# Attention: scaling the exponentials on GpSimd before they are transposed, in place of transposed inverse sums

## What is computed

```
def _masked_softmax(s, mask):
    p = jax.nn.softmax(jnp.where(mask, s, NEG), axis=-1)
    return p * mask.astype(p.dtype)
...
o = g[:, :, 0] * o_cmp + g[:, :, 1] * o_sel + g[:, :, 2] * o_win      # o_sel, o_win: softmax(q k - alibi) v
...
s = (einsum(q_nope, k_nope) + einsum(q_rope, k_r)) * scale             # latent attention
pr = _masked_softmax(s, s_idx[None, :] <= tq[:, None])
return jnp.einsum('bhqs,bshd->bqhd', pr, v)
...
merged = gm[:, :, 0] * (o_nsa @ w_br_nsa[i]) + gm[:, :, 1] * (o_mla @ w_br_mla[i])
```

## Time and profile before

| | |
|---|---|
| median of 3 runs | 1554.8 us (1554.15 to 1554.89) |
| the profiled execution | 1554.5 us, its span 1552.7 us (1.8 us lie around the span) |
| TensorE busy | 1508.3 us, 97% of the span |
| VectorE, ScalarE, GpSimd busy | 665.6, 513.5 and 473.8 us |
| attention loop, first scores of unit 1 to the first merge matmul | 131.09 to 251.28 us from the span's start |

### The profile page before, as it was taken

The page is one execution under the profiler, slowest core; times in us unless marked ns, Lnnn a source line. Parts: engine busy times, 40 slices in busy tenths (PEclk is TensorE's granted clock), DMA queues, the critical chain, the costliest instruction groups (busy, mean ns, idle before and its releaser), DMA issues.

```text
span 1552.7 us, 19377 instructions
## 1 busy us (share of the span) xinstructions
PE 1508.3 (97%) x7613; PEld 1020.4 (66%) x7614; DVE 665.6 (43%) x1102; ACT 513.5 (33%) x917; POOL 473.8 (31%) x249
## 2 busy tenths in 40 slices
PE   8999999999999999999999999999999999998997
PEld 6975667888878888888888777458544343443443
DVE  4155666213643333333343668673633232332334
ACT  4236666222453333331245432524111111111112
POOL 3440125444534444444714355542101000010000
PEclk9999999999999999999999999999999999999999
DMA  8233001222242222222223322257999999999996
GB/s 323 101 117 94 1 2 41 96 95 95 74 143 96 95 95 95 96 99 102 97 82 107 118 76 88 108 197 291 361 430 427 431 422 428 430 429 413 429 426 255
DMA packets 51051, 306.87 MB, mean 198 GB/s; under 512 B 6921, under 2 KB 7177, under 8 KB 38288
## 3 DMA queue, kind: packets, MB, share of 16 engines
q1 hardware_dynamic: 46288, 292.03, 48.0%
q0 software_dynamic: 4096, 11.49, 1.9%
q10 hardware_dynamic: 576, 2.10, 0.3%
HBM read 303.39 MB, written 4.19 MB: 198 GB/s over the span
## 4 chain that ended last, share of the span: by engine, by line
PE 80%; DMA 10%; DVE 5%; ACT 2%; issue 2%; POOL 1%; SPq 0%; ACTq 0%; DVEq 0%; POOLq 0%
PE banks L420 19%; PE banks L465 12%; PE banks L1226 11%; PE banks L423 9%; DMA ring<-experts 8%; PE banks L1270 4%; PE banks L1279 2%; PE banks L445 2%; PE banks L1034 2%; PE banks L2402 2%; PE banks L2483 1%; DMA arena<-experts 1%; PE banks L2418 1%; PE banks L892 1%; PE banks L2389 1%
## 5 line engine op out<-in xcount | busy, mean ns | idle before, releaser
L383 POOL TENSOR_TENSOR arena_r<-ring,arena_r 128x1024 fp32r<-128x1024 f32 x144 | 355.5, 2474 | 411.6 <-ACT arena_r L368 392.1
L368 ACT ACTIVATE arena_r<-ring 128x1024 fp32r<-128x1024 f32 x144 | 151.6, 1058 | 441.0 <-PE banks L423 279.1
L420 PE MATMUL banks<-hT_r,arena_r 128*128 128x512 f32 x640 | 250.0, 391 | 0.0
L420 PE MATMUL banks<-arena_r 128*128 128x512 f32 x640 | 249.1, 389 | 0.0
L1226 PE MATMUL banks<-ring,arena 128*64 128x512 f32 x704 | 222.8, 606 | 14.8 <-DMA ring<-experts 14.7
L465 PE MATMUL banks<-arena_r 128*128 128x512 f32 x784 | 183.5, 389 | 0.6 <-DVE arena_r L410 0.6
L465 PEld LDWEIGHTS banks<-arena_r 128*128 128x128 f32 x784 | 147.1, 188 | 31.5 <-POOL arena_r L383 1.0
L1226 PEld LDWEIGHTS banks<-ring,arena 128*64 128x64 f32 x704 | 70.5, 139 | 145.4 <-issue 144.9
L420 PEld LDWEIGHTS banks<-hT_r,arena_r 128*128 128x128 f32 x640 | 120.1, 188 | 29.0 <-issue 3.4
L420 PEld LDWEIGHTS banks<-arena_r 128*128 128x128 f32 x640 | 120.1, 188 | 25.1 <-issue 0.2
L1894 DVE TENSOR_TENSOR resid<-resid,banks 128x1024 f32<-128x1024 f32 x62 | 72.9, 1217 | 130.5 <-PE banks L1279 130.5
(11 more groups left out here) (491 smaller groups left out, 2129.8 us busy)
## 6 DMA issues: line engine op xcount, KB each, us to landing
ring<-stream SPq DMA_DIRECT2D x164, 512.0 KB, 3.2
arena<-experts SPq DMA_DIRECT2D x37, 2048.0 KB, 15.8
ring<-experts SPq DMA_DIRECT2D x35, 2048.0 KB, 15.5
ring<-experts SPq DMA_DIRECT2D x12, 1024.0 KB, 15.5
arena<-experts SPq DMA_DIRECT2D x12, 1024.0 KB, 17.2
arena<-experts SPq DMA_DIRECT2D x21, 512.0 KB, 9.2
ring<-experts SPq DMA_DIRECT2D x12, 512.0 KB, 6.8
hT<-experts SPq DMA_DIRECT2D x8, 512.0 KB, 11.2
```

Of the source, the lines that this page charges most:

```text
L368: nc.scalar.activation(parts(name, m)[:, 0, :], tile(tile_n), ACT.Copy).then_inc(S["w_high"], 1)
L383: nc.gpsimd.tensor_tensor(w[:, 1, :], tile(tile_n), plain(w[:, 0, :]), ALU.subtract).then_inc(S["w_low"], 1)
L420: nc.tensor.matmul(pb[:, bank, :], w[:, 0, k * P:(k + 1) * P], b[:, k, :], start=(k == 0 and part == 0), stop=False)
```

## The change

GpSimd now multiplies each row of exponentials by its inverse sum (and for kinds 0 and 1 by the gate) in `Pr`, between `exps` and `turn_probs`: two TENSOR_SCALAR instructions per unit, 96 in all, on 128 to 512 columns. The inverse is taken per unit (`invert`, 48 RECIPROCALs of 2 columns in place of 12 of 8). `turn_inverse`, `copy_inverse`, the spread tile and GpSimd's additions to `O_nsa` are gone. The units of kinds 0 and 1 with the same tile and heads now follow each other, and accumulate in one bank (kind 0 starts the sum, kind 1 ends it), so there are 8 `combine`s: four add the bank to `O_nsa`, four copy it to `O_mla`. `turn_probs` and `values` stand one unit later than before against `scores`, and so does `copy_turned` on ScalarE and VectorE. `Pr` has three buffers. The halves of `merge` 0 are formed within the loop, after units 39 to 41, and GpSimd's `nsa_low` after units 43 to 46.

```diff
+            for u in range(N_UNIT):
+                i, kind, pr = UNITS[u]
+                pool.wait_ge(S["at_rinv"], u + 1)
+                for hh in range(2):
+                    p = Pr[u % 3][:, hh, 0:(i + 1) * P]
+                    inverse = sums[:, u, hh:hh + 1]
+                    if kind == 2:
+                        ins = nc.gpsimd.tensor_scalar(out=p, in0=p, scalar1=inverse, scalar2=None, op0=ALU.mult)
+                    else:
+                        at = HEADS * (kind + 1) + 2 * pr + hh
+                        ins = nc.gpsimd.tensor_scalar(out=p, in0=p, scalar1=inverse, scalar2=gates[:, i, at:at + 1],
+                                                      op0=ALU.mult, op1=ALU.mult)
+                    ins.then_inc(S["at_scaled"], 1)
+                if u in (40, 41):
...
+                if 43 <= u < 47:
+                    k = u - 43
+                    pool.wait_ge(S["nsa_hi"], k + 1)
...
             def turn_probs(u):
...
-                    pe.wait_ge(S["at_exp"], 2 * u + hh + 1)
+                    pe.wait_ge(S["at_scaled"], 2 * u + hh + 1)
                     if u:
 
                         pe.wait_ge(S["at_ev_dve"] if hh == 0 else S["at_ev_act"], u)
...
-            for u in range(len(UNITS)):
-                if u + 1 < len(UNITS):
+            for u in range(N_UNIT):
+                if u + 1 < N_UNIT:
                     scores(u + 1)
-                turn_probs(u)
-                if u % 8 == 1 and u > 8:
-                    turn_inverse(u // 8 * 2 - 1)
-                if u % 8 == 7:
-                    turn_inverse(u // 8 * 2)
                 if u:
-                    values(u - 1)
-            values(len(UNITS) - 1)
-            turn_inverse(11)
+                    turn_probs(u - 1)
+                if u >= 2:
+                    values(u - 2)
+            turn_probs(N_UNIT - 1)
+            values(N_UNIT - 2)
+            values(N_UNIT - 1)
...
                 exps(u)
...
-                if u:
-                    copy_turned(u - 1)
+                if u >= 2:
+                    copy_turned(u - 2)
+                if u == 39:
+                    high_act(act, "merge", 0)
...
                 if u:
                     mask_max(u)
-                if u % 8 == 2 and u > 8:
-                    combine(u // 8 * 2 - 1)
-                if u:
-                    copy_turned(u - 1)
...
+                    invert(u - 1)
+                if u >= 2:
+                    copy_turned(u - 2)
+                if u - 3 in SUMS_AT:
+                    combine(u - 3)
```

More of the change, by code:

```diff
@@ L292, in build @@
         xn2 = ar3(10752, NT, D)
-        inverse = [ar(25088 + 512 * b, 512) for b in range(2)]
-        mask = ar(26624, 512)
-        spread = [ar(26112, 512)] * 11 + [junk[:, 0:512]]
+        mask = ar(6144, 512)
         mgt = ar(6656, 4096).rearrange("p (u k c) -> p u k c", u=2, k=4)
@@ L1993, in second_dve @@
                     .then_inc(S["fin_y"], 1)
[L1995 to L1998, removed]
+        UNITS = [(i, kind, pr) for long, short in ((3, 0), (2, 1)) for kinds in ((0, 1), (2,))
+                 for pr in range(4) for kind in kinds for i in (long, short)]
+        N_UNIT = len(UNITS)
+        SUMS_AT = [u for u, (i, kind, pr) in enumerate(UNITS) if kind and pr == 3]
+        FIRST_AT = [u for u, (i, kind, pr) in enumerate(UNITS) if kind != 1 and pr == 0]
         block = ctx.enter_context(nc.Block())
@@ L2079, in _ @@
             nc.gpsimd.tensor_copy(mask[:, T - P:T], cs("diag")).then_inc(S["mask_in"], 1)
[L2080 to L2100, removed]
@@ L2102, in _ @@
+            low_pool(pool, "merge", 1)
             low_pool(pool, "w_o")
@@ L2392, in turn_probs @@
             def turn_probs(u):
-                i, kind, pr, w = UNITS[u]
+                i, kind, pr = UNITS[u]
                 if u == 0:
@@ L2401, in turn_probs @@
                     for kt in range(i + 1):
-                        last = nc.tensor.transpose(pb[:, 4 + hh, kt * P:(kt + 1) * P], Pr[:, u % 2, hh, kt * P:(kt + 1) * P], ident)
+                        last = nc.tensor.transpose(pb[:, 4 + hh, kt * P:(kt + 1) * P], Pr[u % 3][:, hh, kt * P:(kt + 1) * P], ident)
                     last.then_inc(S["at_tr"], 1)
             def values(u):
-                i, kind, pr, w = UNITS[u]
+                i, kind, pr = UNITS[u]
                 if u == 0:
                     pe.wait_ge(S["cs_dve"], 5)
-                if pr == 0 and w >= 2:
-                    pe.wait_ge(S["at_o"], w - 1)
+                if u in FIRST_AT[2:]:
+                    pe.wait_ge(S["at_o"], FIRST_AT.index(u) - 1)
                 pe.wait_ge(S["at_ev_dve"], u + 1)
@@ L2417, in values @@
                             Vsw[:, kt, kind * P + hh * DH:kind * P + hh * DH + DH]
-                        last = nc.tensor.matmul(pb[hh * DH:(hh + 1) * DH, 6 + w % 2, pr * P:(pr + 1) * P], v,
-                                                PTs[:, u % 2, hh, kt * P:(kt + 1) * P], start=(kt == 0), stop=(kt == i))
+                        last = nc.tensor.matmul(pb[hh * DH:(hh + 1) * DH, 6 + u % 2, pr * P:(pr + 1) * P], v,
+                                                PTs[:, u % 2, hh, kt * P:(kt + 1) * P], start=(kt == 0 and kind != 1),
+                                                stop=(kt == i and kind != 0))
                 last.then_inc(S["at_pv"], 1)
[L2422 to L2428, removed]
             pe.wait_ge(S["mla_act"], 7)
@@ L2627, in copy_turned @@
                 nc.scalar.activation(PTs[:, u % 2, 1, 0:nk], pb[:, 5, 0:nk], ACT.Copy).then_inc(S["at_ev_act"], 1)
[L2629 to L2637, removed]
-                if u % 8 == 2 and u > 8:
-                    copy_inverse(u // 8 * 2 - 1)
+            for u in range(N_UNIT):
                 exps(u)
```

97 lines of the change are left out of this document (42 added, 55 removed).

## The result

The changed kernel takes 1559.7 us (median of 6 runs, 1558.5 to 1563.3), the kernel before took 1553.8 beside it (6 runs, 1551.4 to 1554.9): a ratio of 1.004, with a 95% interval of 1.003 to 1.0051. It is slower by 5.9 us. The forecast was 1553.5, no change. The profiled execution of the changed kernel took 1559.1 us, its span is 1557.3.

A forecast was written before the change was run, and what follows sets the result against it. The loop was taken to hang on TensorE, in one of four stretches on scores, row maximum, exponential and ScalarE's copy. Stretches of 37.0, 21.7, 35.7 and 24.5 made 118.9 for 120.19, 1.3 us less: 1553.5 us, range 1550.5 to 1560.

The forecast's parts named there:

- the line: GpSimd scaling price from its copy and cast: 0.18 us + 0.84 per 1000 columns, 0.61 us for 512.
- the upper end: Highest scaling price considered on GpSimd, from TENSOR_TENSOR: 1.27, 0.95, 0.64, 0.32 us for 512 to 128 columns.
- the two-input rival: GpSimd scalings cost two-input prices, 1.27 us per 512 columns, and delay TensorE: 5.0 us more, 1558.5; chance 0.22.
- the last stretch: Loop's fourth part, kind 2 pairs of 384 and 256 columns: three periods of 5.04 and the end, 24.5 for 25.84 us.
- The recorded range: Whole kernel time, 1550.5 to 1560 us, from the main forecast's low end to past the two-input price.
- the third stretch: Loop's pairs of 384 and 256 columns, kinds 0 and 1: seven periods of 4.43, one mixed, 35.7 for 37.55 us.
- ScalarE's copy: Behind two exponentials in ScalarE's queue, it holds TensorE in 512 and 128 column pairs: 5.23 for 4.64, 5.42 for 5.04.
- The end of the loop at the assumed price: Unit 46's scores to the merge: 9.4 us after the change, 9.54 before.
- VectorE's copies not slowed by GpSimd: VectorE's copies out of the banks stay at 692 ns at most beside GpSimd's work; nothing charged.
- the mixed period: One period of 4.7 us, added to seven of 4.43 in the 384 and 256 column pairs of kinds 0 and 1.
- The removed transposes: Twelve turn_inverse of four transposes leave TensorE: 0.5 us each, 6 us in all.
- that `hT_low` sets the merge's pace: Behind the loop, VectorE's hT_low paces the merge despite earlier first weights; this part was taken unchanged.

The follow-up runs named there:

- The trial: The changed kernel plus 20 GpSimd scalings ahead of the loop, 384 and 128 columns in five operand forms; one execution of 1558.4 us.
- the two-column form: The changed kernel with kind 2's scalings also multiplied by a column of ones: 1554.5 us for 1554.1 of the kernel before, ratio 1.0005.
- the cheap form: The changed kernel with kind 2's scalings in two operations, by a column of ones (1554.5 us) or by 1.0 (1554.2 us).
- the constant: The changed kernel with kind 2's scalings also multiplied by a constant 1.0: 1554.2 us for 1552.8 of the kernel before, ratio 1.0005.
- The third such move: VectorE's copy of bank 4 put ahead of its row maxima, on the kernel of 1544.4 us: 1547.2 us.

## Why the prediction was wrong

**The step that failed** is "I take the line, since a scaling too reads one tensor", for the third of the scalings that multiply once. For 384 columns it took 0.50; L2087 measured 1.24 (and 0.92 for 256, where 0.40 was taken). The true price was above the upper end as well. That end held for the forms of two operations only, and for them from 256 columns up. The trial shows the cause as far as it can be seen from outside: the form with one operation has a slope of (1561 - 602) / 384 = 2.5 ns a column, the form with two (766 - 447) / 384 = 0.83, which is the slope of the copy and the cast in the earlier trace rows (0.84). Why the shorter instruction is the slower stays open.

The Trainium skill (GPSIMD Engine Reference, Engine selection) has one-input work on GpSimd at about line rate. For the two-operation form the trace agrees in slope (0.83 ns a column, as for the copy and the cast); for the one-operation form it doesn't (2.5).

**A second step failed with it**: the two-input rival charged the last stretch 0.5 and 1.4 us, from the delay of one unit, and never added up GpSimd's work there. Even at that rival's 0.95 and 0.64 a pair holds 3.2 us of scalings and 1.27 to 2.5 of `mla_low` or `nsa_low`, 4.5 to 5.7 for TensorE's 5.04. At the measured prices it is up to 6.9. So the sign came out as in that rival, by 7.2 us in the last stretch (31.79 for 24.58) where it had 1.9. Of these, about 1 us is TensorE's lower clock, which no step had. The recorded range reached to 1560 for that rival's sake; that 1559.7 lies within it is luck, since the rival took half of its loss from the third stretch, and all of it at two-input prices.

**Right, shown:** ScalarE's copy is what holds the long pairs (5.29 for 5.23, 5.47 for 5.42, and 4.90 and 5.12 once it moves). The end of the loop at the assumed price (9.47 for 9.4). VectorE's copies not slowed by GpSimd.

**Right in mechanism, small in size:** the two-column form costs 0.66 for 384 columns, 0.16 over the line. In the third stretch the scalings thereby come 0.02 us after ScalarE's copy: 4.53, where the copy alone gives 4.51 and the prediction worked out 4.43. The 0.08 are the handover and two transposes. Over the seven periods this is 0.7 of the 1.1 us that the stretch is long; the other 0.36 lie in the mixed period at its start, 5.06 us for the 4.7 taken, and go with the cheap form (4.73). The removed transposes: 3.3 to 3.7 us for three quarters of them, where the prediction's 6 us for all makes 4.5 and the expectation had 4.7.

**Not borne out:** that `hT_low` sets the merge's pace. In the 100 us behind the merge's start TensorE waits for it at most once: 0.26 to 0.54 us in nine of the eleven traces, always 15.6 to 15.8 us behind that start, and not at all in the other two. That what lies behind the loop could be taken unchanged held all the same (1302.3 for 1301.4).

With the price mended, by the constant, the loop takes 120.4 us, against 118.9 forecast, and the kernels with a cheap form take 0.4 and 1.4 us more than the kernel before, where the forecast was 1.3 less: the sum of the other terms held to 1.5 us in the loop and to 2 or 3 in the time.

## What to carry to other kernels

- An operation that the trace does not show can cost more than every neighbour of its kind, and by its form. Price the form that is written, column factor, constant, one or two operations, with a few trial instructions; and when a range is drawn, add up the engine's whole work in each stretch at its upper end, not only the delay of one step.
- Where two waits have nearly one length (4.53 and 4.51 here), each taken away alone shows nothing. Neither null is proof that a wait is free.
- In an in-order queue put first what another engine is waiting for. The cheap form took the loss of 5.9 us away, and no more. ScalarE's copy ahead of the exponentials and VectorE's reciprocal ahead of the next maxima then made a gain of 8.4 of it (1544.4 for 1552.8). The third such move only exchanged one wait for another.

## What the runs showed of the hardware

- GpSimd's TENSOR_SCALAR on fp32, in place: 1.56, 1.24, 0.92 and 0.60 us for 512, 384, 256 and 128 columns with one multiplication by a column; 0.77, 0.66, 0.56 and 0.45 with two by columns; 0.69, 0.58, 0.48 and 0.37 with a column and a constant. A second multiplication by the constant 1.0, which changes nothing, makes it 1.6 times as fast at 128 columns and 2.3 times at 512.
- The one-operation trial by a constant took 1.98 us the first time and 1.33 the second; only four such were run.
- TensorE's granted clock fell to 0.79 and then 0.52 in five-microsecond pieces, where it idled for GpSimd for 0.46, 1.21 and 0.32 us between 245 and 250, and was back at 1.00 in the next piece. No single wait in that stretch was longer than 1.21 us.
- It also fell without any pause of TensorE: in five of eleven profiled executions, to 0.50 to 0.66 on the mean of 110 to 115 us, within or right behind 64 matmuls of 31 columns. The eight long matmuls that follow then took 5.1 to 6.7 us for 3.7.
